# Latent attention scores: 64 own rows of two heads as two row tiles, 32 turned rows as four

## What is computed

```
q = (cq @ w_uq).reshape(B, T, MLA_HEADS, MLA_NOPE + MLA_ROPE)            # 64 + 32
k_nope, v = kv[..., :MLA_NOPE], kv[..., MLA_NOPE:]
k_rope = jnp.broadcast_to(k_rope, (B, T, MLA_HEADS, MLA_ROPE))           # the same for each head
k = jnp.concatenate([k_nope, k_rope], axis=-1)
s = jnp.einsum('bqgrd,bkgd->bgrqk', qi, k) * 96 ** -0.5                  # 128 queries at a time
p = softmax(s);  o = p @ v
```

## Time and profile before

| | before |
|---|---|
| median of 3 runs | 5058.47 us (5057.96 to 5058.73) |
| the profiled execution | 5058.85 us, span 5057.1 us |
| mean granted TensorE clock | 0.970 |
| PE busy | 4712.7 us, 93% |
| DVE busy | 2108.9 us, 42% |
| ACT busy | 1322.0 us, 26% |
| score matmuls (L845) | 407.5 us busy, 1200 records |
| maxima (L931) | 294.4 us busy, 216, mean 1366 ns |
| exponentials (L902) | 266.3 us busy, 216, mean 1233 ns |

### The profile page before, as it was taken

One profiled execution on the slowest core, in us unless ns is written; L12 is line 12 of the kernel. 1 busy time (PEld: TensorE's weight loads), 2 busy tenths in 40 slices (PEclk: granted clock), 3 DMA queues, 4 the chain that ended last, 5 costly groups with the idle time before them and its releaser, 6 DMA issues. The chain is left out here.

```text
span 5057.1 us, 47552 instructions
## 1 busy us (share of the span) xinstructions
PE 4712.7 (93%) x19438; PEld 2523.5 (50%) x19438; DVE 2108.9 (42%) x3552; ACT 1322.0 (26%) x2014; POOL 22.7 (0%) x45
## 2 busy tenths in 40 slices
PE   8899699889799699898999999999999999999996
PEld 2455266665444266753445774555544444444442
DVE  0107455551106455531398231333320355556554
ACT  1100544440200544521311240333320121110023
POOL 0000000000000000000000000000000000000000
PEclk9999799999899799999999999999999999999998
DMA  6000000003011000011011001000001211111111
GB/s 277 25 30 29 4 1 1 1 1 108 29 38 37 4 1 1 1 41 42 21 38 38 30 26 34 17 17 17 17 25 37 79 50 42 50 42 42 67 46 62
DMA packets 43085, 185.81 MB, mean 37 GB/s; under 512 B 4688, under 2 KB 4688, under 8 KB 40720
## 3 DMA queue, kind: packets, MB, share of 16 engines
q1 hardware_dynamic: 36288, 151.01, 8.5%
q0 software_dynamic: 6608, 32.11, 1.7%
HBM read 173.67 MB, written 9.44 MB: 36 GB/s over the span
## 5 line engine op out<-in xcount | busy, mean ns | idle before, releaser
L405 PE MATMUL psum<-arena 128*128 128x512 f32 (+1 forms) x3088 | 1223.6, 558 | 59.7 <-ACTq L389 43.6
L405 PEld LDWEIGHTS psum<-arena 128*128 128x128 f32 x3088 | 585.5, 190 | 696.0 <-issue 681.7
L1812 PE MATMUL psum<-arena 128*128 128x512 f32 x1736 | 746.5, 591 | 1.1 <-DVE arena L2102 1.1
L1812 PEld LDWEIGHTS psum<-arena 128*128 128x128 f32 x1736 | 327.6, 189 | 419.8 <-issue 416.4
L845 PE MATMUL psum<-arena 64*128 64x512 f32 (+3 forms) x1200 | 407.5, 538 | 18.0 <-ACT arena L800 14.1
L931 DVE TENSOR_REDUCE arena<-psum 128x1 f32<-128x1280 f32 (+1 forms) x216 | 294.4, 1366 | 65.4 <-PE psum L845 65.4
L854 PE MATMUL psum<-arena 128*128 128x128 f32 x1968 | 292.8, 279 | 21.1 <-ACT arena L907 19.8
L854 PEld LDWEIGHTS psum<-arena 128*128 128x128 f32 x1968 | 226.6, 141 | 169.9 <-issue 112.8
L902 ACT ACTIVATE arena<-psum,arena 128x1280 f32<-128x1280 f32 (+1 forms) x216 | 266.3, 1233 | 140.5 <-DVE arena L931 136.4
L1785 PE MATMUL psum<-arena 128*128 128x512 f32 x640 | 285.1, 606 | 17.5 <-ACT arena L1919 14.4
L2102 DVE TENSOR_TENSOR arena<-arena,psum 128x512 f32<-128x512 f32 x224 | 154.1, 688 | 301.2 <-PE psum L1812 295.5
(11 more groups left out here) (245 smaller groups left out, 4382.7 us busy)
## 6 DMA issues: line engine op xcount, KB each, us to landing
arena<-stream SPq DMA_DIRECT2D x240, 512.0 KB, 3.5
arena<-mod_w SPq DMA_DIRECT2D x12, 2048.0 KB, 24.1
arena<-x POOLq DMA_DIRECT2D x16, 640.0 KB, 15.6
x_mid<-arena POOLq DMA_DIRECT2D x8, 640.0 KB, 3.4
arena<-x_mid POOLq DMA_DIRECT2D x8, 512.0 KB, 4.2
out<-arena POOLq DMA_DIRECT2D x2, 2048.0 KB, 7.5
arena<-par_a POOLq DMA_DIRECT2D x2, 1449.5 KB, 11.5
arena<-tables POOLq DMA_DIRECT2D x1, 1536.0 KB, 73.8
```

The source lines that it names most:

```text
L405: last = nc.tensor.matmul(ps(slot * SLOT + c0, n), lhsT=sb(w + k * P, P), rhs=rhs(k, c0, n), start=k == 0, stop=k == nk - 1)
L1812: last = nc.tensor.matmul(ps(pair_bank(j, p), HALF), lhsT=lhsT(k), rhs=rhs(k), start=k == 0, stop=k == nk - 1)
```

## The change

Latent scores are made in two parts that add up in PSUM. The own features of a pair's two heads now lie in one block, head 0 in partitions 0 to 63 and head 1 in 64 to 127 (`KM_AT`, `QN_AT`), and their matmuls contract over 64 partitions each ("nope": start, no stop). The turned keys lie four times over 128 partitions (`KR4_AT`), the turned queries of a pair twice (`QR_AT`, 32 rows each, in the order head 0, head 1, head 0, head 1), and their matmuls contract over 32 partitions ("rope": no start, stop), for two heads and up to two chunks of keys side by side. `score_chunks` gives a full latent step five chunks: own 512 of both heads, own 512 of both, turned 512 + 512 of both (four matmuls), own 256 of both, turned 256 of both (two). The score semaphores of both heads are raised in the last one. `act_heads` copies 128 partitions at once for keys and queries; the waits for the projections and the turned queries are placed anew. Grouped-query steps have the same chunks as before.

```diff
--- before.py
+++ after.py
@@ -136,7 +136,8 @@
 U_SEG = T + 2 * PAD
 U_LEN = U_SEG + C + 2 * PAD
 MODW_AT, MODW, MODBUF = Y_AT, 8 * 512, 5
-QM_AT = [U_AT, U_AT + TC, KR_AT, GV_AT]
+QN_AT, QR_AT = [U_AT, KR_AT], [U_AT + TC, GV_AT]
+KR4_AT = KM_AT + 2 * TC
 TAB_AT = U_AT + 2 * U_LEN
 T2_AT = TAB_AT + NTAB
 TMP_AT = T2_AT + T
@@ -703,7 +704,7 @@
 
     def act_rope(t, l):
         for b in range(4):
-            nc.scalar.activation(sb(KM_AT + b * TC + T, C, 64, 96), sb(KR_AT + T, C, 0, 32), ACT.Copy)
+            nc.scalar.activation(sb(KR4_AT + T, C, 32 * b, 32 * b + 32), sb(KR_AT + T, C, 0, 32), ACT.Copy)
         for j in range(10):
             t.eng.wait_ge(v_done[j % 2].sem, t.next(v_done[j % 2]))
             nc.scalar.activation(sb(VM_AT + j * MH * MV, MH * MV), ps(BANK6 + 512 * (j % 2), MH * MV), ACT.Copy)\
@@ -714,14 +715,14 @@
             nc.scalar.activation(sb(VG_AT + j0 * P, n), ps(BANK6 + 512 * (b % 2), n), ACT.Copy).then_inc(v_moved[b % 2].sem, 1)
         t.eng.wait_ge(k_turned.sem, t.next(k_turned))
         for b in range(1, 4):
-            nc.scalar.activation(sb(KM_AT + b * TC, T, 64, 96), sb(KM_AT, T, 64, 96), ACT.Copy)
+            nc.scalar.activation(sb(KR4_AT, T, 32 * b, 32 * b + 32), sb(KR4_AT, T, 0, 32), ACT.Copy)
 
     def dve_rope(t, l):
         table = TAB_AT + TAB["mla"]
         nc.vector.tensor_tensor(sb(TMP_AT, T, 0, 32), sb(KR_AT, T, 0, 32), sb(table, T, 0, 32), ALU.mult)
         nc.vector.tensor_tensor(sb(TMP_AT + TC, T, 0, 32), sb(KR_AT, T, 64, 96), sb(table, T, 64, 96), ALU.mult).then_inc(dve_step.sem, 1)
         t.eng.wait_ge(dve_step.sem, t.next(dve_step))
-        nc.vector.tensor_tensor(sb(KM_AT, T, 64, 96), sb(TMP_AT, T, 0, 32), sb(TMP_AT + TC, T, 0, 32), ALU.add).then_inc(k_turned.sem, 1)
+        nc.vector.tensor_tensor(sb(KR4_AT, T, 0, 32), sb(TMP_AT, T, 0, 32), sb(TMP_AT + TC, T, 0, 32), ALU.add).then_inc(k_turned.sem, 1)
         t.eng.wait_ge(k_turned.sem, t.next(k_turned))
         for i, at in enumerate([GK_AT, GQ_AT, GQ_AT + TC, GQ_AT + 2 * TC]):
             table = TAB_AT + TAB["gqa_cos"]
@@ -751,8 +752,12 @@
 
         wide = chunks(step[4] * P)
         if step[0] == "mla":
-            return [[(s, c0, n)] for s in range(2) for c0, n in wide]
-        return [[(s, c0, n) for s in range(2)] for c0, n in wide]
+            plan = []
+            for i in range(0, len(wide), 2):
+                plan += [[("nope", s, c0, n, 0) for s in range(2)] for c0, n in wide[i:i + 2]]
+                plan.append([("rope", s, c0, n, j) for j, (c0, n) in enumerate(wide[i:i + 2]) for s in range(2)])
+            return plan
+        return [[("all", s, c0, n, 0) for s in range(2)] for c0, n in wide]
 
     def turn_groups(step):
 
@@ -786,20 +791,15 @@
     def act_heads(t, l, p):
         width = layer_shapes(l)
         t.eng.wait_ge(proj_done[0].sem, t.next(proj_done[0]))
-        for s in range(2):
-            last = nc.scalar.activation(sb(KM_AT + (2 * (p % 2) + s) * TC, TC, 0, 64), ps(0, TC, 64 * s, 64 * s + 64), ACT.Copy)
-        last.then_inc(prep_moved[0].sem, 1)
+        nc.scalar.activation(sb(KM_AT + p % 2 * TC, TC), ps(0, TC), ACT.Copy).then_inc(prep_moved[0].sem, 1)
         if width > T:
             t.eng.wait_ge(proj_done[1].sem, t.next(proj_done[1]))
             for s in range(2):
-                last = nc.scalar.activation(sb(QM_AT[2 * (p % 2) + s] + T, C, 64, 96), ps(SLOT + T, C, 32 * s, 32 * s + 32), ACT.Copy,
+                last = nc.scalar.activation(sb(QR_AT[p % 2] + T, C, 64 * s, 64 * s + 64), ps(SLOT + T, C, 0, 64), ACT.Copy,
                                             scale=MQ ** -0.5)
             last.then_inc(prep_moved[1].sem, 1)
         t.eng.wait_ge(proj_done[0].sem, t.next(proj_done[0]))
-        for s in range(2):
-            last = nc.scalar.activation(sb(QM_AT[2 * (p % 2) + s], width, 0, 64), ps(0, width, 64 * s, 64 * s + 64), ACT.Copy,
-                                        scale=MQ ** -0.5)
-        last.then_inc(prep_moved[0].sem, 1)
+        nc.scalar.activation(sb(QN_AT[p % 2], width), ps(0, width), ACT.Copy, scale=MQ ** -0.5).then_inc(prep_moved[0].sem, 1)
 
     def dve_heads(t, l, p):
         table = TAB_AT + TAB["mla"]
@@ -809,8 +809,7 @@
             .then_inc(dve_step.sem, 1)
         t.eng.wait_ge(dve_step.sem, t.next(dve_step))
         for s in range(2):
-            r = (32 * s, 32 * s + 32)
-            nc.vector.tensor_tensor(sb(QM_AT[2 * (p % 2) + s], T, 64, 96), sb(T1_AT, T, *r), sb(T2_AT, T, *r), ALU.add)\
+            nc.vector.tensor_tensor(sb(QR_AT[p % 2], T, 64 * s, 64 * s + 64), sb(T1_AT, T, 0, 64), sb(T2_AT, T, 0, 64), ALU.add)\
                 .then_inc(q_turned[s].sem, 1)
 
 
@@ -827,23 +826,28 @@
 
         def scores(u, chunk):
             kind, p, tile, k0, nkt, _ = steps[u]
-            for s, c0, n in chunk:
+            for part, s, c0, n, j in chunk:
                 if u:
                     prob(s, u - 1)
-                if waiting[s]:
-                    if s == 0:
-                        t.eng.wait_ge(prep_moved[0].sem, t.next(prep_moved[0]))
-                        if l == 0:
-                            t.eng.wait_ge(prep_moved[1].sem, t.next(prep_moved[1]))
-                    t.eng.wait_ge(q_turned[s].sem, t.next(q_turned[s]))
-                    waiting[s] = False
-                if kind == "mla":
-                    q, keys = sb(QM_AT[2 * (p % 2) + s] + tile * P, P, 0, MQ), sb(KM_AT + (2 * (p % 2) + s) * TC + k0 * P + c0, n, 0, MQ)
+                if waiting[0] and part == "nope":
+                    t.eng.wait_ge(prep_moved[0].sem, t.next(prep_moved[0]))
+                    waiting[0] = False
+                if waiting[1] and s == 1:
+                    if l == 0:
+                        t.eng.wait_ge(prep_moved[1].sem, t.next(prep_moved[1]))
+                    for half in range(2):
+                        t.eng.wait_ge(q_turned[half].sem, t.next(q_turned[half]))
+                    waiting[1] = False
+                r = (64 * s, 64 * s + 64)
+                if part == "nope":
+                    q, keys = sb(QN_AT[p % 2] + tile * P, P, *r), sb(KM_AT + p % 2 * TC + k0 * P + c0, n, *r)
+                elif part == "rope":
+                    r = (64 * j + 32 * s, 64 * j + 32 * s + 32)
+                    q, keys = sb(QR_AT[p % 2] + tile * P, P, *r), sb(KR4_AT + k0 * P + c0, n, *r)
                 else:
-                    r = (64 * s, 64 * s + 64)
                     q, keys = sb(GQ_AT + p * TC + tile * P, P, *r), sb(GK_AT + k0 * P + c0, n, *r)
-                last = nc.tensor.matmul(ps(s * SLOT + c0, n), lhsT=q, rhs=keys, start=True, stop=True)
-                if c0 + n == nkt * P:
+                last = nc.tensor.matmul(ps(s * SLOT + c0, n), lhsT=q, rhs=keys, start=part != "rope", stop=part != "nope")
+                if c0 + n == nkt * P and part != "nope":
                     last.then_inc(score_done[s].sem, 1)
 
         def turn(u, g, tiles):
```

## The result

The changed kernel takes 5200.15 us (median of 4 runs, 5194.49 to 5200.8) against 5058.6 us for the kernel before: a ratio of 1.0279, with a 95% interval of 1.0264 to 1.0294. It is slower by about 141 us. The forecast was 5240, with a range of 5155 to 5345.

What follows compares the result with a forecast made beforehand. PE alone was taken to pace the latent step. Regular steps 151, odd steps 13 + 13 + 7 + 4 and copies -6 sum to +182 us on 5058.85: 5241, given as 5240 (68%), range 5155 to 5345.

Steps and rivals of the forecast that it cites:

- What paces the step: Latent step: PE alone paces its 9.27 us; with the change it becomes 13.04 us although 0.85 us of columns are saved.
- The price of a visit: Latent scores: each way into row tiling and out costs 0.58 us for two tiles, 1.00 for four.
- the stagger: Row-tiled scores: tiles start 0.26 us apart; 0.21 counted as each further tile's price, 0.05 as a semaphore wait.
- stagger gone: Rival: switches are paid but tiles start together, 1.48 us less per regular step, 5176 us in all; 7%.
- The tail taken from the grouped-query step: Latent step's end: 4.72 us from the maximum's start to the next scores, both exponentials inside, as in grouped-query steps.
- The regular steps: Full latent steps with full scores behind them: 40 in two layers, each +3.77 us, 151 in all.
- The odd steps: Latent layers: behind context steps +13, layer starts +13, six intervals with context scores +7, two before a new head pair +4 us.
- The copies: act_heads: one copy of 128 partitions instead of two shortens the projection wait by 1.2 or 0.8 us, -6 in all.
- The clock: Rival: slower, idler PE gets a clock of 0.85 over 540 us of PE-paced time, +95, 5335 us; 10%.
- The free switches: Rival: entering and leaving row tiling costs nothing and tiles start together; step 9.9 us, 5089 in all; 4%.
- the four tiles in sequence: Rival: turned-key matmuls on four row tiles don't run together, +2.1 us on about 43 steps, 5332 in all; 9%.
- the faster case: Rival: the saved columns reach the end, 45 us less, 5014 in all; 2%.

Runs made afterwards that it cites:

- b_rows64: Kernel before, with latent score matmuls over the 64 own rows only, turned rows left out, same order and columns: 5169.44 us, ratio 1.0222.
- b_order: Kernel before, with a latent step's chunks taken from both heads in turn, no row tiling, same columns: 5138.21 us, ratio 1.0158.
- b_joint: Kernel before, with PE waiting for both exponentials at once ahead of a grouped-query step's first score matmul: 5063.55 us in one run.
- a_two_late: Changed kernel with the same matmuls in two visits to row tiling, two transposing groups between own and turned chunks: 5097.9 us, ratio 1.008.
- a_two: Changed kernel with the same matmuls in two visits to row tiling, one transposing group between own and turned chunks: 5130.18 us, ratio 1.0142.
- a_ahead: Changed kernel with all own, then all turned chunks of a latent step ahead of its five transposing groups: 5122.1 us, ratio 1.0124.
- a_moves: Changed kernel with DVE's move 3 ahead of the maximum and ACT's move 4 ahead of the exponential in latent steps: 5159.32 us, ratio 1.0202.
- b_late: Kernel before, with grouped-query steps' scores put between the second and third transposing group, latent steps unchanged: 5026.67 us, ratio 0.9938.

## Why the prediction was right, and where it was off

**What paces the step, and that columns saved there are not time saved: right.** b_rows64 and b_order show the two causes apart, 1.70 and 1.39 us a step. Added up, less 0.85 of columns, they make 2.24 of the 2.62. The change has two things more that neither run has: the 0.26 us wait of the second head in the first chunk, and a values' wait of 1.59 us instead of 1.31.

**The price of a visit: too high.** I had 0.58 us for two tiles and 1.00 for four; the trace has 0.35 for either (1.06 and 1.08 us to the group behind it). The term that failed is the stagger. I took 0.21 of the 0.26 us between the two starts of the earlier trace rows as the price of each further tile, and put only 0.05 of it down to a semaphore. b_joint shows that it was the semaphore wait altogether. All four of the changed kernel's first turned records together take 0.71 us, against 0.69 for one of them:

```profile
1978.32 0.69 PE L849 MATMUL psum<-arena 32*128 32x512 f32 x1
1978.32 0.71 PE L849 MATMUL psum<-arena 32*128 32x512 f32 x4
```

From the first chunk to the maximum's start I had 8.27 us; it is 7.16 (1974.77 to 1981.93), and that is nearly all of the 1.15 us by which the step was too long. The rival "stagger gone" was therefore the right one on this point, and its step (13.04 - 1.48 = 11.56) is nearer to 11.89 than mine. It missed by 0.33, of which 0.21 is the second exponential's wait, which both had at 0.05 and which is 0.26 in the first chunk. Its total of 5176 is nearer too, 24 us below the measured time where the forecast is 40 above. So what the Trainium skill says in "TensorE: Matmul & The Clock Gate", Part 3, of the starts of packed matmuls (about 4 ns apart) holds for f32 here, and I was wrong to say that the trace disagreed: the starts in b_joint are 0.01 us apart. That a change of mode drains the engine, as the Trainium skill has it in "TensorEngine Tiling (Array Packing)", Key Properties, agrees with b_rows64, where such changes cost 1.70 us a step.

**The tail taken from the grouped-query step: right.** 4.72 us from the maximum's start to the next scores; the changed kernel has 4.73 (1981.93 to the next scores at 1986.66), and a_two_late, a_two and a_ahead fit it as well. The reason given, move 3 behind top(0), is what a_moves took away, and its 0.60 us shows a second wait right behind that the prediction had inside the 4.72.

**The regular steps: size off.** Predicted were 40 intervals at 3.77 us, 151 in all, less the copies of four of them. Measured are 107: 36 without a head pair give 101 (31 at 2.6, five at 3.9 to 4.0) and the four with one give 6.

**The odd steps.** Behind the two context steps +17 (13 predicted, part of it at the lower clock), the two starts of a layer +11 with their copies (11 without the rounding), the nine intervals around context steps +5 (11 predicted). The hand-over to grouped-query attention gave 2, and grouped-query attention itself gave back 1.7 behind its context steps, with less time at the lower clock. Together with the 107 that is the 141 us measured.

**The copies: right in mechanism, and in size at the place that was looked at.** Their removal cost more in all, with the clock as the open part.

**The clock: a small part of the rival came.** Five regular steps took 13.2 to 13.3 us instead of 11.89, like this one, from values to values, with a grant of 0.87:

```profile
849.71:862.98 13.27, 11.68 (x88) 7.59 (x88) 5.31 (x10) 4.51 (x8) 0.00 (x0) 0.87 0.01 1
```

That is 5 x 1.36 = 7 us of the 141, and some more in the intervals behind context steps (0.79 to 0.84); the rival had 95. The sum of the forecast had nothing for it, so part of the nearness of 182 to 141 is luck: without the lower clock the gap would be wider by these 7 us and more. The free switches, the four tiles in sequence and the faster case are excluded by the rows above.

## What to carry over

When matmuls are split to fill the array, count the changes of mode first: a way in and out had the same price here for two tiles and for four, for 512 columns and for 256 (0.35 us), and five of them cost twice the columns that were saved. Then ask which of the outputs completes last, and what is queued behind its reader. Two heads finished together take away the cover that one head finished early gives (1.39 us a step in b_order). Where such a tail sets the step, place the block of scores behind the group whose copy would otherwise stand ahead of the maximum: one group's difference in place was worth 0.76 us a step between a_two and a_two_late, with the same matmuls. Before reading a gap between two starts as the price of hardware, look for a semaphore wait between them.

## What the runs showed of the hardware

- Row tiles start together: 0.71 us for four first records of 512 columns where one takes 0.69, and two likewise in b_joint.
- Two tiles that start apart stay apart for the visit, as its length shows: in the earlier trace rows it is 2.61 us with starts 0.26 apart, which is the 2.35 of the scores in b_late (2056.22 to 2058.57) and the 0.26.
- A way from 128 rows into 64 or 32 rows and back costs 0.35 us: 0.20 in the chunk (1.06 for 0.853) and 0.15 in the group behind it (0.58 for 0.435).
- In b_rows64 the granted clock fell behind a wait of PE to the lower of its two levels, 1.2 GHz of 2.4, and stayed there for 20 to 27 us in which PE had no idle time at all (0.68 over the 30 us from 640). The kernel before, with matmuls of 96 rows, had the lower level for 3.4 us behind the same wait. What differs is contraction over 64 rows, one tile at a time, and a change of mode at each chunk; which of the two matters was not tried. Even together they do not bring the clock down by themselves: once it was full, the same work kept 1.00 for 156 us.
